# A three-layer fp32 network on one core: banks carried between phases, two split tiles on VectorE, an out projection cut four and four, and planned steps moved

## The chip, the cores and the metric

The kernel runs on one core of a Trainium2 chip. The metric is the device time of one launch in microseconds (us). Before the change three runs took 1080.02, 1081.88 and 1081.51 us, median 1081.51.

## What is computed

256 tokens of 1024 features, fp32, pass through three layers. Each has an RMS norm, an input projection, a mixer, an output projection added to x, a second norm, and a gated feed-forward network of width 2816 added to x.

```
layer 0: u = rms(x) @ w_in; o = silu(g) * rms(retention(q, k, v))        6 heads
layer 1: u = rms(x) @ w_in; o = rms(diff_attention(q, k, v, lam))        6 heads
both:    x += concat(o, memory_attention(rms(qc), mk, mv)) @ w_out       4 memory heads
layer 2: y_ssd = rms(ssd(conv4(xbc), dt) * silu(z)); y_fox = fox_attention(rms(q), rms(k), v)
         x += concat(y_ssd, y_fox) @ w_out                               16 + 16 heads
all:     x += (silu(gate) * value) @ w_down                              conv3 before it in layer 2
```

Layer 1's diff attention takes softmax p0 - lam * p1 of two score maps per head. All matrices are multiplied nearly exactly: weights and activations are each split into a rounded high part and a low part (the rest), and three of the four products are summed.

## The kernel before, in words

**Phases and tiles.** The program is a row of phases (PHASES): kv, and for each layer in, oa, ob, up, down. A phase walks weight tiles; an output of 128 features by 256 tokens needs one tile of 8 blocks (24 matmuls in `project`, L701 to L703, three per block) or, in oa and down, fewer or more blocks. Weights stream through a ring of four slots: SyncE loads a tile, ScalarE rounds it (`split_hi`, L1077), VectorE subtracts (`split_lo`, L1535), three tiles ahead of TensorE; SyncE reloads a slot when its low part is done.

**Banks.** Each output is summed in a PSUM bank. In in and oa phases outputs alternate between banks 0 and 1, in the other phases between 0 to 3, and each phase starts again at bank 0 (`phases`, `Phase.bank`). TensorE may start an output when VectorE has evacuated the last one in that bank. in0 and in1 have 17 outputs, in2 has 41, so these phases end in bank 0, and oa begins there.

**Out projection.** It runs in two phases: oa takes the inputs that are there early, ob the late ones. In layer 0 oa0 has six inputs (8 tiles of 6 blocks, 18 matmuls each) and ob0 two inputs, four outputs to a ring tile. In layer 1 it is four (8 tiles of 4 blocks) and four (two outputs to a ring tile). ob also computes the next norm's inputs: per output VectorE adds to x (L1633), ScalarE makes the high part and the square (L1082, L1088), GpSimd sums squares (L1460), VectorE makes the low part (L1541).

**The plan.** The mixer runs between tiles. `plans` gives for each layer and slot (one slot per ring tile of in, then of oa; slot 20 is the first of oa in layers 0 and 1, slot 45 in layer 2) a list of steps; every engine does its part of a step in list order. TensorE does its steps after the tile of the slot, or for the kinds in HALFWAY in the middle of the next tile. VectorE does the kinds in EARLY before it evacuates the slot's tile, MIDDLE after that and before the split, LATE after the split. ScalarE does its steps after its split of the slot. So one long wait on an engine holds all that is queued behind it, evacuations and splits too.

**Steps that matter here.** A `norm` is squares (ScalarE), sums (TensorE L809), roots by Ln and Exp (ScalarE L1211, L1213), five VectorE operations (L1724 to L1740), a `spread` (TensorE L818) and `norm_out` (VectorE L1752 or L1749). An attention unit is scores, maxima (VectorE L1788, L1799 or L1908), exponentials (ScalarE L1260, L1338), normalization (`softmax`, VectorE L1822 to L1835 and ScalarE L1280; `fox_probs`, L1915 and L1347), transposes of the weights (TensorE L944 or L917, copied by ScalarE L1270 or L1359), values (TensorE L843, L928, copied by VectorE L1848). `mix` splits one mixed tile into the inputs of the out projection: ScalarE rounds (L1294), GpSimd subtracts (L1488). `gated` is layer 0's product with silu(g) (L1779). In layer 2 `turn` transposes convolved tiles (TensorE L832), `small` prepares decays (its last step: TensorE L988), `z_silu` is one silu over eight tiles (L1372), and for head pair p come ssd_decay (L999, L1000, L1328), ssd_weights (VectorE L1887), ssd_out (TensorE L1011), ssd_skip (L1902), ssd_gate (L1926) and ssd_square. `fox_scores` is on TensorE L904 (fp32r), L908 (plain fp32), L911 (fp32r).

The pieces on which most hangs:

```
HALFWAY = ((), ("spread",), ("spread", "ssd_out"))
EARLY = {"norm_out", "softmax", "ssd_weights", "ssd_skip", "fox_probs"}
MIDDLE = {"group_out", "gated_soon"}
planned = sorted(planned, key=lambda step: step[0] in ("ssd_skip", "norm_out"))   # layers 1, 2, EARLY
```

Of the kernel before, what the change touches and what calls it, by code (L numbers as in the profile page):

```python
# [23 lines left out]
P = 128  # L24
T = 256
# [21 lines left out]
OUT_INPUTS = {"oa0": [6, 7, 0, 1, 2, 3], "ob0": [4, 5], "oa1": [6, 7, 0, 1], "ob1": [2, 3, 4, 5],  # L47
# [68 lines left out]
class Phase:  # L116
# [33 lines left out]
    def bank(self, i, c):  # L150

        return (self.out(i if type(i) is int else 0, c) - self.out0) % self.banks
# [11 lines left out]
def phases():  # L164

    at, out, all_, widths, bank_of = 0, 0, {}, [], []
    for name, n, blocks, body in PHASES:
        p = all_[name] = Phase(name, n, blocks, body, at, out)
        p.bank_of = bank_of
        bank_of += [j % p.banks for j in range(p.outs)]  # L170
# [5 lines left out]
def plans():  # L176
# [7 lines left out]
    def norm(layer, slot, tile, soon=False):  # L184
# [4 lines left out]
        plan[layer][slot + 2].insert(0, ("spread_soon" if soon or slot >= 20 and layer == 1 else "spread", tile))  # L189
# [14 lines left out]
    def mem_pairs(layer):  # L204

        for pair in range(2):
# [21 lines left out]
    norm(0, 15, 39)  # L228
    norm(0, 17, 41)
    for half_, slot, kind in ((0, 18, "gated"), (1, 19, "gated_soon"), (2, 20, "gated")):  # L230
        at(0, 20 if half_ == 2 else 18, "gate_silu", half_)
        at(0, slot, kind, half_)
    for half_, slot in ((0, 19), (1, 19), (2, 20)):
        at(0, slot, "mix", 2 * half_)
        at(0, slot, "mix", 2 * half_ + 1)


    for t, slot in ((18, 2), (0, 3), (6, 5), (2, 7), (8, 9), (4, 13), (10, 15), (8 + 64, 20)):
        norm(1, slot, t)
    norm(1, 16, 6 + 64, True)  # L240
    norm(1, 23, 10 + 64, True)
# [3 lines left out]
    for h, slots in enumerate(((9, 10, 11, 12), (11, 12, 13, 14), (13, 14, 15, 18), (15, 16, 17, 19),  # L245
                               (18, 19, 20, 21), (20, 21, 21, 22))):
# [4 lines left out]
        at(1, turned, "weights", "diff", h)  # L251
    for h, slot in enumerate((9, 11, 13, 15, 18, 20)):
        for m in range(2):
            at(1, slot, "scores", "diff", h, m)
    for k, slot in ((0, 19), (1, 19), (2, 23), (3, 23), (4, 26), (5, 26)):
        at(1, slot, "mix", k)


    for t in range(8):
        at(2, 3 + t, "turn", 8 + t)  # L260
    at(2, 13, "cb", 0)
    for s, slot in enumerate((13, 14, 14, 15, 15)):
        at(2, slot, "small", s)
    at(2, 21, "z_silu", 0)
# [10 lines left out]
    for j in range(4):  # L275
# [3 lines left out]
        for n in range(2):  # L279
# [3 lines left out]
            at(2, slot + 2, "fox_weights", p)  # L283
            at(2, slot + 3, "fox_values", p)
# [1831 lines left out]
```

## Time and profile before

| what | value |
|---|---|
| median of three runs | 1081.51 us |
| the profiled execution's own time | 1080.11 us |
| its span, first to last instruction | 1078.0 us |
| mean granted TensorE clock | 0.998 of full speed |
| TensorE busy (matmul) | 1046.7 us, 97% |
| VectorE busy | 746.3 us, 69% |
| ScalarE busy | 602.0 us, 56% |
| GpSimd busy | 165.7 us, 15% |
| read from HBM | 172.39 MB |

Busy time is the union of an engine's instructions. Matmuls are pipelined: one record is 0.28 us long, but in a full stream the next starts 0.12 us later. The distance of starts tells the pace. An idle time in square brackets stands before an instruction, with what ended it; "issue" means that nothing in the profile shows it. The profiled run is 1.4 us faster than the median.

### The profile page before, as it was taken

How to read it: one execution, taken by the hardware profiler on the slowest of the kernel's cores; microseconds unless marked ns; L12 is line 12 of the kernel's file. 1: busy time of each engine (PE TensorE's matmuls, PEld its weight loads, DVE VectorE, ACT ScalarE, POOL GpSimd, SP SyncE). 2: the span in 40 equal slices, each digit the busy share in tenths (PEclk: the TensorE clock that was granted, in tenths of full speed). 3: DMA queues.
4: the chain of work that ended last, by engine and by line, in shares of the span. 5: the costliest groups of instructions: out<-in, count | busy, mean ns of one | idle time of the engine just before them, and what ended most of it. 6: DMA issues, size and time to landing. Idle time of an engine off the chain costs nothing.

```text
span 1078.0 us, 23843 instructions
## 1 busy us (share of the span) xinstructions
PE 1046.7 (97%) x8638; PEld 1008.5 (94%) x8638; DVE 746.3 (69%) x1242; ACT 602.0 (56%) x1091; POOL 165.7 (15%) x172
## 2 busy tenths in 40 slices
PE   6999999999999998999999999999999999999998
PEld 6989999999999887899999998989888899999998
DVE  6875686666555887866665548867867479988743
ACT  7654564444544766654445446665766566666532
POOL 3200121111110000511111110000101033544300
PEclk9999999999999999999999999999999999999999
DMA  7533455555665332555555664534232355555563
GB/s 290 175 130 110 138 174 189 178 183 178 187 175 184 130 99 76 179 178 191 177 178 175 189 199 139 177 136 138 90 118 89 121 194 187 182 181 188 163 205 102
DMA packets 51479, 174.43 MB, mean 162 GB/s; under 512 B 5840, under 2 KB 7120, under 8 KB 51280
## 3 DMA queue, kind: packets, MB, share of 16 engines
q1 hardware_dynamic: 51408, 173.46, 49.9%
q8 instruction: 48, 0.79, 0.3%
q14 instruction: 23, 0.19, 0.1%
HBM read 172.39 MB, written 1.05 MB: 161 GB/s over the span
## 4 chain that ended last, share of the span: by engine, by line
PE 52%; DVE 5%; ACT 2%; issue 1%; POOL 0%; ACTq 0%; DVEq 0%
PE bank L701 10%; PE bank L702 9%; PE bank L703 9%; PE scores L703 6%; PE scores L702 6%; PE scores L701 6%; DVE ring_lo L1535 1%; ACT tmp L1338 1%; DVE xw_lo L1541 1%; PE scores L908 1%; PE bank L928 1%; PE scores L917 0%; DVE negmax L1908 0%; PE bank L1011 0%; PE bank L684 0%
## 5 line engine op out<-in xcount | busy, mean ns | idle before, releaser
L1535 DVE TENSOR_TENSOR ring_lo<-ring_raw,ring_hi 128x1024 fp32r<-128x1024 f32 (+2 forms) x338 | 402.0, 1192 | 59.1 <-ACT ring_hi L1077 53.2
L1077 ACT ACTIVATE ring_hi<-ring_raw 128x1024 fp32r<-128x1024 f32 (+2 forms) x338 | 341.3, 1012 | 87.2 <-PE bank L703 49.4
L701 PE MATMUL bank<-xw_hi,ring_hi 128*128 128x256 f32 x1048 | 303.2, 289 | 2.7 <-DVE ring_lo L1535 1.5
L702 PE MATMUL bank<-xw_lo,ring_hi 128*128 128x256 f32 x1048 | 296.3, 283 | 0.0
L703 PE MATMUL bank<-xw_hi,ring_lo 128*128 128x256 f32 x1048 | 296.2, 283 | 0.0
L701 PEld LDWEIGHTS bank<-xw_hi,ring_hi 128*128 128x128 f32 x1048 | 200.5, 191 | 9.7 <-issue 5.1
L702 PEld LDWEIGHTS bank<-xw_lo,ring_hi 128*128 128x128 f32 x1048 | 200.7, 191 | 0.2
L703 PEld LDWEIGHTS bank<-xw_hi,ring_lo 128*128 128x128 f32 x1048 | 200.6, 191 | 0.0
L701 PE MATMUL scores<-xw_hi,ring_hi 128*128 128x256 f32 x528 | 149.4, 283 | 0.0
L702 PE MATMUL scores<-xw_lo,ring_hi 128*128 128x256 f32 x528 | 149.4, 283 | 0.0
L703 PE MATMUL scores<-xw_hi,ring_lo 128*128 128x256 f32 x528 | 149.4, 283 | 0.0
L701 PE MATMUL bank<-act_hi,ring_hi 128*128 128x256 f32 x464 | 134.7, 290 | 11.3 <-DVE ring_lo L1958 7.4
L703 PE MATMUL bank<-act_hi,ring_lo 128*128 128x256 f32 x464 | 132.4, 285 | 0.0
L702 PE MATMUL bank<-act_lo,ring_hi 128*128 128x256 f32 x464 | 132.4, 285 | 0.0
L701 PEld LDWEIGHTS bank<-act_hi,ring_hi 128*128 128x128 f32 x464 | 90.1, 194 | 14.2 <-DVE ring_lo L1958 7.4
L701 PEld LDWEIGHTS scores<-xw_hi,ring_hi 128*128 128x128 f32 x528 | 101.4, 192 | 0.0
L702 PEld LDWEIGHTS scores<-xw_lo,ring_hi 128*128 128x128 f32 x528 | 101.4, 192 | 0.0
L703 PEld LDWEIGHTS scores<-xw_hi,ring_lo 128*128 128x128 f32 x528 | 101.4, 192 | 0.0
L1148 ACT ACTIVATE act_hi<-tmp 128x256 f32 (+1 forms) x66 | 27.2, 413 | 132.5 <-DVE tmp L1657 130.0
L1464 POOL TENSOR_TENSOR act_lo<-tmp,act_hi 128x256 f32 (+1 forms) x66 | 53.6, 812 | 264.1 <-ACT act_hi L1148 264.1
L702 PEld LDWEIGHTS bank<-act_lo,ring_hi 128*128 128x128 f32 x464 | 90.2, 194 | 0.0
L703 PEld LDWEIGHTS bank<-act_hi,ring_lo 128*128 128x128 f32 x464 | 90.1, 194 | 0.0
(236 smaller groups left out, 1773.8 us busy)
## 6 DMA issues: line engine op xcount, KB each, us to landing
ring_raw<-w_up SPq DMA_DIRECT2D x132, 512.0 KB, 3.2
ring_raw<-w_in SPq DMA_DIRECT2D x85, 512.0 KB, 3.2
ring_raw<-w_down SPq DMA_DIRECT2D x48, 512.0 KB, 3.6
ring_raw<-w_down SPq DMA_DIRECT2D x24, 384.0 KB, 3.8
ring_raw<-w_ob SPq DMA_DIRECT2D x10, 512.0 KB, 3.3
ring_raw<-w_oa SPq DMA_DIRECT2D x16, 256.0 KB, 2.7
ring_raw<-w_oa SPq DMA_DIRECT2D x8, 512.0 KB, 3.5
ring_raw<-w_kv SPq DMA_DIRECT2D x7, 512.0 KB, 6.6
```

What stands on the lines that cost most here:

```text
L701: mm(bank[b][:, 0:T], w_hi, tile(hi, t), start=kk == 0, stop=False)
L702: mm(bank[b][:, 0:T], w_hi, tile(lo, t), start=False, stop=False)
L703: last = mm(bank[b][:, 0:T], w_lo, tile(hi, t), start=False, stop=end)
L908: mm(bank[2 + n][:, a:a + width], u[r0:r0 + 64, q0 * T + it * P:q0 * T + (it + 1) * P], u[r0:r0 + 64, k0 * T:k0 * T + width], start=False, ...
L928: last = mm(bank[6][64 * n:64 * n + 64, q:T], tok(v_tok, (2 * p + n) * 64, 64, tt), fox_pt(n)[:, tt * T:tt * T + width], start=tt == 0, st ...
L1077: A(ring_hi[:, slot * DM:slot * DM + width], ring_raw[:, slot * DM:slot * DM + width], ACT.Copy).then_inc(hi_done, 1)
L1148: A(tile(act_hi, f), two(prod, h), ACT.Copy).then_inc(ffn_hi, 1)
L1338: last = A(fox_p(n)[:, a:a + width], bank[2 + n][:, a:a + width], ACT.Exp, bias=negmax[:, c:c + 1], accum_out=rowsum[:, c:c + 1])
L1464: G.tensor_tensor(tile(act_lo, f), two(prod, h), tile(act_hi, f).bitcast(f32), SUB).then_inc(ffn_lo, 1)
L1535: V.tensor_tensor(ring_lo[:, a:b], ring_raw[:, a:b], ring_hi[:, a:b].bitcast(f32), SUB).then_inc(lo_done, 1)
L1541: V.scalar_tensor_tensor(tile(lo, m), tile(src, m), pcol(name, m), tile(hi, m).bitcast(f32), MUL, SUB).then_inc(xl_done, 1)
```

## The change

Nothing is computed otherwise; steps are placed otherwise.

1. **Banks**: a phase begins with the bank after the last one of the phase before (`shift`).
2. **Out projection of layer 0**: four and four inputs, as in layer 1. oa0 has 12 matmuls to a tile, ob0 four ring tiles of two outputs.
3. **Low parts of mixed tiles in layers 0 and 1**: `mix` on single tiles becomes `mix_high` (ScalarE, two tiles at once) and `mix_low` (VectorE, two at once) in place of GpSimd. Layer 2 keeps `mix`.
4. **Layer 0**: spreads move to the middle of the next tile; the transposes of memory heads 0 and 2 too, their copy one slot later. The gate product of half 0 goes to slots 17 and 18 and its split to 18 and 19; halves 1 and 2 go to slots 20 to 23. `gate_silu` 0 brings the Ln and Exp table back, so there are two more table loads.
5. **Layer 1**: the first pair's split moves from slot 19 to 18. Head 5's scores on TensorE move from slot 20 to 19 and its maxima stay in 20; its transposes move from after tile 21 to the middle of tile 23, copy and values to slot 23. The norm of tiles 8 and 9 is spread and applied one slot later, that of tiles 10 and 11 in slot 26 instead of 25, before the split. Scores of head h wait for the maxima of the head before (VectorE) and not for its exponentials (ScalarE).
6. **Layer 2**: turns one slot later; the last small step in the middle of tile 16; ssd_gate not before slot 22, ssd_square not before 23. The EARLY order puts norm_out ahead of fox_probs where a slot has both. Transposes of fox pairs 6 and 7 move to the middle of the next tile, values of pair 7 one slot later. `fox_scores` does L908 before L904.

```diff
-          ("in0", 20, [8], 20), ("oa0", 8, [6], 8), ("ob0", 2, [8], 2), ...
+          ("in0", 20, [8], 20), ("oa0", 8, [4], 8), ("ob0", 4, [8], 4), ...
-OUT_INPUTS = {"oa0": [6, 7, 0, 1, 2, 3], "ob0": [4, 5], ...
+OUT_INPUTS = {"oa0": [6, 7, 0, 1], "ob0": [2, 3, 4, 5], ...
-        return (self.out(i if type(i) is int else 0, c) - self.out0) % self.banks
+        return (self.out(i if type(i) is int else 0, c) - self.out0 + self.shift) % self.banks
+        p.shift = (bank_of[-1] + 1) % p.banks if bank_of else 0
+        bank_of += [(j + p.shift) % p.banks for j in range(p.outs)]
...
-                at(layer, slot + 1 + n, "weights", "mem", 2 * pair + n)
+                if layer == 0 and n == 0:
+                    at(layer, slot + 1, "turned", "mem", 2 * pair)
+                    at(layer, slot + 2, "weights_copy", "mem", 2 * pair)
...
+    at(0, 18, "mix_high", 0)
     norm(0, 17, 41)
+    at(0, 17, "gate_silu", 0)
+    at(0, 18, "gated_early", 0)
+    at(0, 19, "mix_low_early", 0)
+    for half_ in (1, 2):
+        at(0, 20, "gate_silu", half_)
+        at(0, 20 + half_, "gated", half_)
+        at(0, 21 + half_, "mix_high", 2 * half_)
+        at(0, 21 + half_, "mix_low", 2 * half_)
...
-                               (18, 19, 20, 21), (20, 21, 21, 22))):
+                               (18, 19, 20, 21), (20, 21, 22, 23))):
+    for m in range(2):
+        at(1, 19, "scores_ahead", "diff", 5, m)
+        at(1, 20, "maxima", "diff", 5, m)
+    for k, slot in ((2, 24), (4, 26)):
+        at(1, slot, "mix_high", k)
+        at(1, slot, "mix_low", k)
...
-        at(2, 3 + t, "turn", 8 + t)
+        at(2, 4 + t, "turn", 8 + t)
-        at(2, a + 3, "ssd_gate", p)
-        at(2, max(a + 4, 22), "ssd_square", p)
+        at(2, max(a + 3, 22), "ssd_gate", p)
+        at(2, max(a + 4, 23), "ssd_square", p)
...
+            def mix_low(layer, k):
+                dve.wait_ge(pair_hi, number_low(layer, k) + 1)
+                t = mixed_tile(None, layer, k)
+                V.tensor_tensor(tile(act_lo, k, 2 * T), tile(u, t, 2 * T), tile(act_hi, k, 2 * T).bitcast(f32),
+                                SUB).then_inc(pair_lo, 1)
...
+            HALFWAY = (("spread", "turned"), ("spread", "turned"), ("spread", "ssd_out", "small_turn", "fox_turned"))
+                        probs_wait = any(step[0] == "fox_probs" for step in planned)
+                        last = ("ssd_skip", "fox_probs") if probs_wait else ("ssd_skip", "norm_out")
```

## Rows read from the trace of the kernel before

**Rows 1.** Page, parts 1 and 6: TensorE's busy time; loads of 256 KB, us to landing
```profile
PE 1046.7 (97%) x8638; PEld 1008.5 (94%) x8638; DVE 746.3 (69%) x1242; ACT 602.0 (56%) x1091; POOL 165.7 (15%) x172
...
ring_raw<-w_oa SPq DMA_DIRECT2D x16, 256.0 KB, 2.7
```

**Rows 2.** Waits of TensorE: waiting line <- releaser: us in total, times, longest
```profile
PE bank L809 <- DVE u L1752: 2.2, 3, 1.2
PE bank L944 <- ACT tmp L1280: 1.9, 1, 1.9
PE bank L1011 <- DVE con L1887: 1.8, 1, 1.8
PE bank L818 <- DVE root_parts L1740: 1.6, 3, 0.9
...
PE scores L917 <- ACT tmp L1347: 1.3, 2, 0.9
...
PE bank L944 <- DVE tmp L1828: 1.1, 1, 1.1
...
PE bank L988 <- DVE scratch L1872: 1.0, 1, 1.0
...
PE bank L832 <- issue: 0.8, 1, 0.8
```

**Rows 3.** Stretches, layer 0's tail, TensorE alone: length, busy (matmuls), clock, DMA, GB/s
```profile
117.50:120.00 2.50, 1.37 (x9) 0.99 0.14 22
120.00:122.50 2.50, 2.50 (x13) 0.50 0.34 135
122.50:125.00 2.50, 2.50 (x19) 0.83 0.20 54
```

**Rows 4.** Stretches: length, busy (count) of PE, PEld, DVE, ACT, POOL, clock, DMA, GB/s
```profile
126.00:140.00 14.00, 14.00 (x119) 14.00 (x118) 9.91 (x15) 6.41 (x8) 0.00 (x0) 1.00 0.72 225
144.00:149.00 5.00, 3.91 (x25) 3.15 (x25) 4.97 (x11) 4.12 (x9) 3.78 (x5) 1.00 0.33 105
454.00:458.00 4.00, 3.90 (x31) 3.56 (x30) 3.82 (x7) 3.19 (x6) 3.18 (x3) 1.00 0.49 165
419.00:444.00 25.00, 19.52 (x153) 16.68 (x152) 19.53 (x46) 15.53 (x35) 6.63 (x6) 1.00 0.43 139
```

**Rows 5.** Timeline of ScalarE, slot 20 of layer 0
```profile
118.92 0.62 ACT L1246 ACTIVATE u<-u 128x512 f32<-128x512 f32 x1
119.55 1.28 ACT L1061 ACT_TABLE_LOAD   x1
```

**Rows 6.** Timeline of VectorE, slots 21 and 22 of layer 1
```profile
429.22 0.36 DVE L1724 SCALAR_TENSOR_TENSOR bank<-bank,par,tmp 128x128 f32<-128x128 f32 x1 [0.53 <-ACT tmp L1213]
...
430.80 0.42 DVE L1848 COPY u<-bank 128x256 f32<-128x256 f32 x1
...
431.46 0.68 DVE L1535 TENSOR_TENSOR ring_lo<-ring_raw,ring_hi 128x512 fp32r<-128x512 f32 x1
```

**Rows 7.** Timeline of VectorE at the start of layer 2's turns
```profile
663.12 0.42 DVE L1663 TENSOR_TENSOR con<-bank,rstd 128x256 f32<-128x256 f32 x1 [0.27 <-PE bank L703]
```

**Rows 8.** Timeline of ScalarE, slot 21 of layer 2
```profile
720.18 1.91 ACT L1372 ACTIVATE u<-u 128x2048 f32<-128x2048 f32 x1
...
723.40 0.73 ACT L1328 ACTIVATE tmp<-bank,tmp 128x256 f32<-128x256 f32 x2
```

**Rows 9.** Timeline of VectorE, slot 20 of layer 2
```profile
722.19 0.42 DVE L1926 TENSOR_TENSOR u<-u 128x256 f32<-128x256 f32 x1 [3.74 <-ACT u L1372]
```

**Rows 10.** Timeline of ScalarE ahead of TensorE's longest wait at L809
```profile
770.74 0.64 ACT L1206 ACTIVATE tmp<-u 128x512 f32<-128x512 f32 x1
```

**Rows 11.** Timeline of TensorE, that wait
```profile
772.24 0.43 PE L809 MATMUL bank<-tmp,con 128*32 128x128 f32 x8 [1.20 <-DVE u L1752]
```

**Rows 12.** Timeline of TensorE, first two parts of one fox_scores
```profile
781.37 0.62 PE L904 MATMUL scores<-act_hi,pick_r 128*128 128x384 f32 x2
781.92 0.93 PE L908 MATMUL scores<-u 64*128 64x128 f32 x8
```

More of the change, by code:

```diff
@@ L188, in norm @@
         at(layer, slot + 1, "norm", tile)
-        plan[layer][slot + 2].insert(0, ("spread_soon" if soon or slot >= 20 and layer == 1 else "spread", tile))
+        plan[layer][slot + 2].insert(0, ("spread_soon" if soon else "spread", tile))
         if soon:
@@ L228, in plans @@
     norm(0, 15, 39)
+    at(0, 18, "mix_high", 0)
     norm(0, 17, 41)
[L230 to L238, printed above, removed]
+    at(0, 17, "gate_silu", 0)
[6 more added lines that the diff above has]
+        at(0, 21 + half_, "mix_low", 2 * half_)
+    for t, slot in ((18, 2), (0, 3), (6, 5), (2, 7), (8, 9), (4, 13), (10, 15)):
         norm(1, slot, t)
     norm(1, 16, 6 + 64, True)
-    norm(1, 23, 10 + 64, True)
+    for t, slot in ((8 + 64, 20), (10 + 64, 23)):
+        at(1, slot, "squares", t)
+        at(1, slot + 1, "norm", t)
+    plan[1][23].insert(0, ("spread", 8 + 64))
+    plan[1][24].insert(0, ("norm_out", 8 + 64))
+    at(1, 26, "spread_soon", 10 + 64)
+    at(1, 26, "norm_mid", 10 + 64)
     mem_pairs(1)
@@ L504, in program @@
                     k = (layer, *key)
-                    count("norm" if kind == "group_norm" else kind, (kind, *k) if kind in ("norm", "group_norm") else k)
+                    same = {"group_norm": "norm", "weights_copy": "weights", "maxima": "scores"}
+                    count(same.get(kind, kind), (kind, *k) if kind in ("norm", "group_norm") else k)
                     if kind == "norm":
@@ L901, in fox_scores @@
                 blocks_ = [(0, 0, P), (1, P, T)]
-                for n in range(2):
-                    pick = pick_r[:, 16 + 2 * p + n:17 + 2 * p + n].to_broadcast([P, P])
-                    mm(bank[2 + n][:, 0:T + P], pick, small_r[:, 0:T + P], start=True, stop=False)
                 for it, a, width in blocks_:
@@ L908, in fox_scores @@
                         mm(bank[2 + n][:, a:a + width], u[r0:r0 + 64, q0 * T + it * P:q0 * T + (it + 1) * P],
-                           u[r0:r0 + 64, k0 * T:k0 * T + width], start=False, stop=False)
+                           u[r0:r0 + 64, k0 * T:k0 * T + width], start=it == 0, stop=False)
+                for n in range(2):
+                    pick = pick_r[:, 16 + 2 * p + n:17 + 2 * p + n].to_broadcast([P, P])
+                    mm(bank[2 + n][:, 0:T + P], pick, small_r[:, 0:T + P], start=False, stop=False)
                 for n in range(2):
@@ L1294, in mix, with mix_high @@
                 A(tile(act_hi, k), tile(u, t), ACT.Copy).then_inc(mix_hi, 1)
+            def mix_high(layer, k):
+                t = mixed_tile(act, layer, k)
+                A(tile(act_hi, k, 2 * T), tile(u, t, 2 * T), ACT.Copy).then_inc(pair_hi, 1)
             def c_times_b(layer, _):
@@ L1941, in follow @@
                 return steps
-            EARLY = {"norm_out", "softmax", "ssd_weights", "ssd_skip", "fox_probs"}
-            MIDDLE = {"group_out", "gated_soon"}
+            EARLY = {"norm_out", "softmax", "ssd_weights", "ssd_skip", "fox_probs", "gated_early", "mix_low_early"}
+            MIDDLE = {"group_out", "norm_mid"}
             LATE = set(DO) - EARLY - MIDDLE
```

69 lines of the change are left out of this document (43 added, 26 removed), and 2 rows, old and new, of the table PHASES.

## Prediction

> **What bounds it now.** I read the page first. TensorE is busy for 1046.7 of 1078.0 us [rows 1], so the change can only win what lies in the other 31.3 us, plus what a matmul loses while it counts as busy. The number of matmuls stays the same: layer 0's out projection has 8 x 18 + 2 x 24 = 192 before and 8 x 12 + 4 x 24 = 192 after. VectorE (69%) and ScalarE (56%) are not the bound of the whole, but one of them ends most waits. So the second view is the list of TensorE's waits [rows 2]: eight entries that the change aims at, each some 1 to 2 us in total. The third is a table of stretches, since a wait can cost more than itself.
>
> That table has one surprise [rows 3]. In layer 0's tail the granted clock falls to 0.50, which is the lower of TensorE's two levels (1.2 instead of 2.4 GHz), after a stretch in which it worked for only 1.37 of 2.50 us. 9 + 13 + 19 = 41 matmuls take 7.5 us there. At full pace, 14.00 us for 119 matmuls or 0.118 us each [rows 4], they take 4.8. So 2.7 us are lost, 1.1 as idle time (2.50 - 1.37) and 1.6 by the clock. By the Trainium skill ("TensorE: Matmul & The Clock Gate", Part 1) the clock follows how busy the engine has been, which agrees with these rows.
>
> **Layer 0.** (a) oa0's first tile needs four inputs instead of six, the split of the pair it lacks is moved ahead into slots 18 and 19, and oa0 begins in the bank that in0 left free. The 2.7 us go, and I add 0.4 for the bank, between nothing and the 0.8 that a wait on nothing visible takes elsewhere [rows 2]. What comes back: ScalarE's slot 20 now holds two silus and two table loads. A load takes 1.28 and a silu 0.62 us [rows 5], with its split 4.4 us in all, while a tile of 12 matmuls takes 12 x 0.118 = 1.4. The split for tile 24 is queued behind that, VectorE's low part behind the split, and behind this the evacuation of tile 22, the gate products and both low parts. TensorE reaches tile 24 some 6.1 us after oa0's start, VectorE frees its bank some 0.5 later, and the two products and two low parts of 0.6 us each hold tile 25 for some 0.7 more. I take 1.2 back; the ends are 0 and 2.7. Net 1.9. By the Trainium skill ("ScalarE: Activation LUTs", What ACT_TABLE_LOAD costs) each switch takes about 2.66 us with its drain. The row has 1.28 with the next instruction 1.3 after; by the page slot 20 would be 2.8 us longer, and the total some 2.8 us higher.
> (b) up0's start is VectorE-bound: 144 to 149 us holds 25 matmuls in 5.0 us (2.1 lost), while up1 after four-input groups holds 31 in 4.0 (0.3 lost) [rows 4]. ob0 gets layer 1's shape, so 1.7 us is won. SyncE issues two loads more; loads of 256 KB land in 2.7 us [rows 1], and each has four tiles, 5.7 us, from its slot's release to its use. I cost them at nothing, with that distance as their cover; without it each would show its 2.7.
> (c) The transposes of memory head 0 wait 1.1 us for VectorE [rows 2]. Half a tile later they don't, but their copy now stands behind a split on ScalarE and the next transposes want that bank: 0.3 back, net 0.8 (ends 0 and 1.1). Spreads in the middle of a tile win some 0.3 of the 1.6 at L818 [rows 2]; the rest is layer 1's.
> Layer 0: 1.9 + 1.7 + 0.8 + 0.3 = 4.7.
>
> **Layer 1.** From 419 to 444 us TensorE is busy 19.52 of 25 us: 5.5 us of waits [rows 4]. All seem to be removed, but VectorE is busy 19.53 of the same 25 and gets two low parts more in it, some 0.6 each by the 0.68 of a low part of the same width [rows 6]. I walked its queue. Head 5's scores move ahead, so its maxima, exponentials and softmax end some 1.5 us sooner. Then the norm of tiles 8 and 9 (waits 0.53 for ScalarE's roots, 429.22), head 4's values (430.80) and only then the evacuation and split (431.46) follow in the old order [rows 6]. TensorE, with its transposes moved away, now arrives early and waits there: about 0.5 for the bank of tile 21, 1.3 for head 4's values to leave bank 6, and, since the last norm is applied in slot 26 behind an evacuation and its low part behind a 1024-wide split, 1.6 in ob1's first output. That makes some 3.4 of which pipelining hides part of what it hid before; the difference I take is 3.0 (ends: 0.5, if VectorE's added 1.2 and a later last norm eat the rest, and 5.5). Head 5's wait on maxima instead of exponentials adds no wait: maxima come first.
>
> **Layer 2.** (d) Turns. The first waits 0.8 us [rows 2], for the copy of the norm's roots that VectorE makes in slot 3. A slot later that is done. But from there VectorE idles only 0.27 us per slot or less [rows 7]: TensorE's lead runs into convolutions that aren't ready, and each turn waits for ScalarE's copy of the one before. I take 0.5 (ends 0 and 0.8).
> (e) The last small step waits 1.0 us at L988 [rows 2] and moves 12 matmuls, 1.4 us, back: 1.0 (ends 0.5 and 1.0). Its copies on ScalarE are wanted only in slot 17.
> (f) ssd_out waits 1.8 us at L1011 [rows 2]. ScalarE's silu over eight tiles ends at 722.09 [rows 8], and VectorE stands 3.74 us before ssd_gate, with ssd_weights queued behind it [rows 9]. With the gate in slot 22 VectorE goes on. Late next is ssd_decay 5 on TensorE, which wants the exponential of decay 4, queued on ScalarE behind silu and load and done at 724.13 [rows 8], when TensorE arrives at about 723.8: 0.4 back, net 1.4 (ends 0.5 and 1.8).
> (g) norm_out ahead of fox_probs: 2.2 us at L809 in three waits [rows 2]. The longest ends at 772.24 and began 1.20 sooner, at 771.04 [rows 11]. But L809 also wants the squares, which end at 771.38 [rows 10], so only 0.8 of 1.2 goes; the others, 0.5 each, go: 1.8. Late fox_probs cost nothing, since ScalarE's next work is a split.
> (h) Fox transposes 6 and 7: 1.3 us [rows 2] in two waits, of which 0.1 stays behind the same ScalarE work: 1.1 with some for the values (ends 0.6 and 1.3).
> (i) Order in fox_scores. L904's two matmuls of 384 columns should take 2 x 1.5 x 0.118 = 0.35 us and take 0.55 before L908 starts [rows 12]: a change between fp32r and plain fp32 costs some 0.1 to 0.2. Seven of eight fox_scores follow plain fp32 values, and with L908 first they change once instead of three times: 7 x 0.17 = 1.2 (ends 0 and 2.4).
> Layer 2: 0.5 + 1.0 + 1.4 + 1.8 + 1.1 + 1.2 = 7.0.
>
> **Sum.** 4.7 + 3.0 + 7.0 = 14.7 us. The profiled execution took 1080.11, so it would take 1065.4; it is 1.4 faster than the median 1081.51, which gives 1066.8. I put the forecast between the two: 1066.
>
> **Rivals.** 1. VectorE is the bound of both tails. For: 19.53 of 25 us busy, and added work. Against: GpSimd's 6.63 us in that stretch [rows 4] go in part, and VectorE idles where it waits for ScalarE. Price: layer 1 keeps 0.5, (a) 0.5, (c) 0, (d) 0, (g) to (i) half: 1.7 + 0.5 + 0.5 + 0.3 + 1.0 + 1.4 + 2.0 = 7.4, time 1074.
> 2. No new waits: layer 0 gives 2.7 + 0.4 + 1.7 + 1.1 + 0.3 = 6.2, layer 1 5.5, layer 2 0.8 + 1.0 + 1.8 + 2.2 + 1.3 + 2.4 = 9.5: 21.2 us, time 1060. Against it is the queue on VectorE.
> 3. Slower: the clock stays at its lower level through both out projections. The waits that I leave in slots 24 and 25 of layer 0 and in slots 22 to 28 of layer 1 come again with nearly every tile. 13 matmuls in 2.50 us are 0.192 each against 0.118 [rows 3, 4], near the lower level's double; 192 matmuls in each tail cost 14 us, both 28, and 28 - 14.7 is 13 slower, 1094. [...] Against: my waits are 1.6 of several us at most, and layer 1's 5.5 of 25 us did not lower it [rows 4]. [...]
> 4. The longer table load of the page: 1069, inside the forecast's range.
> 5. The change doesn't do what it says: the low part isn't earlier because ScalarE's mix_high waits for a late norm_out. Then only layer 2 and (b) hold: 8.7, time 1073, near rival 1.
>
> **Chances.** Forecast 0.60, rival 1 (with 5) 0.20, rival 2 0.11, rival 3 0.03, rival 4 0.06. The range, 1060 to 1075, holds all but rival 3 and the edges. A measurement of this kernel tells about 0.2%, 2.2 us, from no change. Faster by over that: 0.95; within 0.02, slower 0.03.
>
> **What would show it.** In the changed profile: clock 1.00 all through layer 0's tail; the wait for GpSimd's act_lo in oa0 gone; up0's start at layer 1's pace; waits at L1011, L988 and L809 gone or under 0.6; a wait of some 1.5 us in ob1's first output, now on VectorE's low part; L908 straight after L928. I am wrong if a stretch of out projection shows a clock under 0.9, if VectorE's splits (ring_lo) come to lead TensorE's waits, or if TensorE's busy time plus idle time falls by less than 7.

## The result, and the profile after

The changed kernel takes **1065.94 us** (median of four runs, 1065.02 to 1066.21), the kernel before 1081.70 (four runs beside it, 1080.02 to 1082.60). The ratio is 0.9855, interval 0.9838 to 0.9872: 15.8 us less, where the forecast was 1066. The profiled execution took 1066.21 us with a span of 1064.4, 13.9 us less than the profiled execution before. The other 1.9 us have a likely source in the clock. Of 35 executions of the kernel before that were timed beside the experiments, 18 have a mean granted clock of 0.997 and take 1082.1 us on average, 14 have 0.998 (the profiled one too) and take 1080.6, and two have 1.000 and take 1079.3. The changed kernel has 1.000 in all four.

The page of the changed kernel, parts 1 and 2 (the clock in 40 slices) and part 6 (loads of up and ob; the last number is us to landing):

```profile
PE 1042.4 (98%) x8638; PEld 1007.9 (95%) x8638; DVE 749.8 (70%) x1250; ACT 604.4 (57%) x1089; POOL 155.9 (15%) x160
...
PEclk9999999999999999999999999999999999999999
...
ring_raw<-w_up SPq DMA_DIRECT2D x132, 512.0 KB, 3.2
...
ring_raw<-w_ob SPq DMA_DIRECT2D x12, 512.0 KB, 4.1
```

The span is 1078.0 - 1064.4 = 13.6 us shorter. TensorE is busy 4.3 us less with the same 8638 matmuls [rows 1], so 9.3 are idle time. Where it went is best read from stretches cut at the same instructions in both kernels. The cuts are the starts of the mean squares (L743 before, L780 after), of oa and ob (the first matmul that reads act_hi, and L724 or L761), of the product of C and B (L839, L876), and of decays 0 and 7 (L999, L1036). In this order the stretches are: in0; oa0 with ob0; in1; oa1; ob1; layer 2's turns; its small steps; decays 0 to 7; and the rest up to the next mean square.

Three of these stretches in the kernel before (oa0 with ob0, oa1, the turns): length, busy TensorE (matmuls), clock, share of the DMA engines' time, GB/s.

```profile
116.96:148.94 31.98, 29.35 (x216) 0.95 0.49 157
...
420.07:441.49 21.42, 17.82 (x142) 1.00 0.42 133
...
648.91:691.83 42.92, 41.45 (x334) 1.00 0.46 156
```

The same three in the changed kernel, and the last one.

```profile
114.77:144.51 29.74, 27.83 (x223) 1.00 0.63 196
...
415.55:433.94 18.39, 16.20 (x137) 1.00 0.45 143
...
641.35:684.46 43.11, 40.89 (x335) 1.00 0.46 158
...
723.23:873.47 150.24, 148.73 (x1257) 1.00 0.40 129
```

| stretch | before, us | after, us | won | forecast |
|---|---|---|---|---|
| in0: memory transposes, spreads, and the 0.4 for the bank | 77.17 | 74.85 | 2.3 | 1.5 |
| oa0 and ob0: the rest of (a), and (b) | 31.98 | 29.74 | 2.2 | 3.2 |
| layer 1: in1 | 80.25 | 80.16 | 0.1 | |
| oa1 | 21.42 | 18.39 | 3.0 | 3.0, all of layer 1 |
| ob1 | 16.54 | 16.53 | 0.0 | |
| turns (d) | 42.92 | 43.11 | -0.2 | 0.5 |
| small steps (e) | 14.41 | 13.35 | 1.1 | 1.0 |
| decays 0 to 7, the gate (f) | 26.93 | 25.42 | 1.5 | 1.4 |
| the rest: norm's output, fox transposes, fox order (g, h, i) | 153.84 | 150.24 | 3.6 | 4.1 |
| sum | | | 13.7 | 14.7 |

One line has the wrong sign, and equal sums can hide opposite errors (layer 1 does). in1 and oa1 have to be read together: the change moves head 5's scores, about 1.0 us of TensorE's work, from oa1 into in1 (80.16 us with them there, 79.11 in the experiment below that puts head 5 back), and the 0.87 us that TensorE waited for a bank at the end of in1 are gone. TensorE's waits of the changed kernel (waiting line, releaser: us in total, times, longest), as far as the steps speak of them:

```profile
PE bank L738 <- DVE x L1658: 2.1, 3, 0.9
PE bank L869 <- ACT x_tok L1265: 2.0, 4, 1.2
PE scores L761 <- DVE act_lo L1831: 1.4, 1, 1.4
PE bank L880 <- ACT tmp L1308: 1.1, 1, 1.1
...
PE bank L846 <- ACT tmp L1244: 0.6, 1, 0.6
PE bank L983 <- ACT tmp L1308: 0.3, 1, 0.3
...
PE bank L1048 <- DVE con L1939: 0.2, 1, 0.2
PE bank L855 <- DVE root_parts L1785: 0.2, 1, 0.2
PE scores L956 <- ACT tmp L1391: 0.2, 1, 0.2
```

Against [rows 2], with the line in the changed kernel first: L846 (L809 before) from 2.2 to 0.6, L983 (L944) from 3.0 in two to 0.3, L1048 (L1011) from 1.8 to 0.2, L855 (L818) from 1.6 to 0.2, L956 (L917) from 1.3 to 0.2; the 1.0 at L988 is gone, and so are the waits for GpSimd (1.4 in two at L701 and 1.0 at L724). New are the first four rows. L869 is the turn: from one wait of 0.8 to four, of 2.0 together.

### The profile page after: what moved, and what is told of

The parts are those of the page before. It is cut to its first block, busy times and chain, and to the rows that moved or that the text cites. A ratio compares the mean times of both kernels' runs of the same rounds, so it can differ in the third digit from the quotient of the medians.

```text
span 1064.4 us, 23813 instructions
## 1 busy us (share of the span) xinstructions
PE 1042.4 (98%) x8638; PEld 1007.9 (95%) x8638; DVE 749.8 (70%) x1250; ACT 604.4 (57%) x1089; POOL 155.9 (15%) x160
## 4 chain that ended last, share of the span: by engine, by line
PE 51%; DVE 6%; ACT 3%; issue 1%; ACTq 0%; DVEq 0%
PE bank L738 10%; PE bank L739 9%; PE bank L740 9%; PE scores L738 6%; PE scores L740 6%; PE scores L739 6%; DVE ring_lo L1580 1%; ACT tmp L1382 1%; DVE xw_lo L1586 1%; PE scores L944 0%; PE bank L1048 0%; PE bank L967 0%; DVE negmax L1960 0%; DVE tmp L1717 0%; DVE x L1678 0%
## 5 line engine op out<-in xcount | busy, mean ns | idle before, releaser
L738 PE MATMUL bank<-xw_hi,ring_hi 128*128 128x256 f32 x1048 | 302.6, 289 | 1.9 <-DVE ring_lo L1580 0.6
L738 PEld LDWEIGHTS bank<-xw_hi,ring_hi 128*128 128x128 f32 x1048 | 200.5, 191 | 8.4 <-issue 5.1
L738 PE MATMUL scores<-xw_hi,ring_hi 128*128 128x256 f32 x528 | 150.1, 284 | 0.1
L738 PE MATMUL bank<-act_hi,ring_hi 128*128 128x256 f32 x448 | 129.6, 289 | 9.9 <-DVE ring_lo L2013 7.4
L739 PE MATMUL bank<-act_lo,ring_hi 128*128 128x256 f32 x448 | 127.8, 285 | 0.0
L740 PE MATMUL bank<-act_hi,ring_lo 128*128 128x256 f32 x448 | 127.6, 285 | 0.0
L738 PEld LDWEIGHTS scores<-xw_hi,ring_hi 128*128 128x128 f32 x528 | 101.4, 192 | 0.4 <-DVE xw_lo L1586 0.3
L738 PEld LDWEIGHTS bank<-act_hi,ring_hi 128*128 128x128 f32 x448 | 86.8, 194 | 11.8 <-DVE ring_lo L2013 7.4
L739 PEld LDWEIGHTS bank<-act_lo,ring_hi 128*128 128x128 f32 x448 | 87.0, 194 | 0.0
L740 PEld LDWEIGHTS bank<-act_hi,ring_lo 128*128 128x128 f32 x448 | 86.9, 194 | 0.0
```

Of the source, the lines that this page charges most:

```text
L738: mm(bank[b][:, 0:T], w_hi, tile(hi, t), start=kk == 0, stop=False)
L739: mm(bank[b][:, 0:T], w_hi, tile(lo, t), start=False, stop=False)
L740: last = mm(bank[b][:, 0:T], w_lo, tile(hi, t), start=False, stop=end)
```

## The experiments

### The turns: one slot back, and in the middle of a tile

```diff
-        at(2, 4 + t, "turn", 8 + t)
+        at(2, 3 + t, "turn", 8 + t)        # both kernels
-            ... ("spread", "ssd_out", "small_turn", "fox_turned"))
+            ... ("spread", "ssd_out", "small_turn", "fox_turned", "turn"))    # the second only
```

> The changed kernel with layer 2's turns back in slots 3 to 10. My theory of step (d): after the first turn the stretch is paced by VectorE's convolutions and by ScalarE's copy of the turn before, so the place of the turns hardly matters. From up to the first product of C and B (layer 2's mean square to L1054's kind) the kernel before took 42.9 us and the changed one 43.1; I expect 42.9 here, all later stages as in the changed kernel, total 0.2 us less. Rival (the forecast's step): moving them had won 0.5 to 0.8, then this run is slower by that.

> The changed kernel with each turn in the middle of the next tile (8 to 15 after slots 3 to 10). Theory: a turn waits for ScalarE's copy of the turn before, which comes half a tile too late; with 1.4 us more distance the four waits (2.0 us as idle time, 2.6 in starts) go, and the stretch is limited by TensorE: about 41.0 instead of 43.1 us, total 1.5 to 2.5 us less. Rival: VectorE's convolutions (3.1 us of work per slot against 3.3) are the limit and hold it at 42.5 or more.

**Measured.** One slot back: 1065.51 us (1065.16 to 1065.92), ratio 0.9863 (0.9847 to 0.9880). From the mean square to the product of C and B it takes 42.92 us (640.49 to 683.41), 0.2 less than the changed kernel and the same as before. In the middle: 1062.62 us (1062.38 to 1063.35), ratio 0.9836 (0.9820 to 0.9853), and that stretch is 40.38 us (640.65 to 681.03), 2.7 less. Timeline of TensorE in the changed kernel, the first of the four turns that wait (start, length, and in brackets the idle time before it); the other three wait 0.28 us each:

```profile
658.53 0.41 PE L869 MATMUL bank<-con,u 128*128 128x128 f32 x2 [1.15 <-ACT x_tok L1265]
```

**What follows.** The move took away the first turn's wait of 0.8 us and gave the second turn one of 1.15, for another engine. The transposes of one turn want the bank that ScalarE's copy of the one before leaves, and that copy is queued behind the convolution's silu. Every second turn waits in this way (the second, fourth, sixth and eighth). Half a tile (1.4 us of matmuls) is enough cover: with the turns in the middle no wait at L869 is left at all.

### Layer 1: who does the low parts, and head 5

```diff
-                  "maxima": scores, "norm_mid": norm_out, "mix_low": mix_low, "mix_low_early": mix_low,
+                  "maxima": scores, "norm_mid": norm_out,      # VectorE; mix_low runs on GpSimd, one tile at a time
```

> The changed kernel with the low parts of mixed tiles in layers 0 and 1 on GpSimd again (two of 256 columns each), at the same places of the plan. Theory: a pair takes GpSimd 1.5 to 1.7 us against VectorE's 0.7, but VectorE is freed of it. In layer 0's oa the two waits for banks (0.75 and 0.47) shrink to at most 0.4 in all: oa0 13.7 us goes to 12.9. In layer 1 the last pair is wanted at once: ob1's wait of 1.4 us becomes some 2.0, and the first pair's place makes no wait. Total within 0.5 us of the changed kernel. Rival (VectorE is the bound of both tails): 2 us or more faster. Second rival (the low parts on VectorE are the gain of the change): 2 us or more slower.

```diff
+    norm(1, 20, 8 + 64)
+    norm(1, 23, 10 + 64, True)
...
-                               (18, 19, 20, 21), (20, 21, 22, 23))):
+                               (18, 19, 20, 21), (20, 21, 21, 22))):
...
-    for m in range(2):
-        at(1, 19, "scores_ahead", "diff", 5, m)
-        at(1, 20, "maxima", "diff", 5, m)
...
-    for k, slot in ((2, 24), (4, 26)):
+    for k, slot in ((2, 23), (4, 26)):
```

> The changed kernel with layer 1's head 5 and its two last normalisations put back to their old tiles; the low parts stay pairs on VectorE, and the banks and everything in layers 0 and 2 stay changed. The changed kernel won 3.1 us in layer 1, all of it in the first part of the out projection. If the earlier scores and turned weights of head 5 and the later normalisation are what won it (my theory): layer 1 goes from 115.1 back to 117.6 to 118.2, with waits of 1 to 2 us again at head 5's scores and weights and ahead of the ring's high part, and the time is 1068.5 to 1069. If the pairs on VectorE won it (rival): layer 1 stays below 116 and the time is 1066 to 1067.

**Measured.** Low parts on GpSimd: 1069.54 us (1067.75 to 1069.68), ratio 0.9899 (0.9883 to 0.9916), 3.6 slower in the median. Head 5, both norms and the middle pair's slot back, the pairs still on VectorE: 1065.72 us (1065.18 to 1066.36), ratio 0.9854 (0.9839 to 0.9869): no slower than the changed kernel. TensorE's timeline in layer 1's out projection, first the kernel before:

```profile
420.07 0.35 PE L701 MATMUL bank<-act_hi,ring_hi 128*128 128x256 f32 x1 [0.87 <-issue]
421.38 0.39 PE L701 MATMUL bank<-act_hi,ring_hi 128*128 128x256 f32 x1 [0.35 <-POOL act_lo L1488]
428.65 0.55 PE L944 MATMUL bank<-con,tmp 128*128 128x128 f32 x3 [1.94 <-ACT tmp L1280]
430.94 0.66 PE L818 MATMUL bank<-root_parts,spread_r 128*128 128x128 f32 x4 [0.32 <-DVE root_parts L1740]
438.07 0.66 PE L818 MATMUL bank<-root_parts,spread_r 128*128 128x128 f32 x4 [0.91 <-DVE root_parts L1740]
444.13 0.39 PE L724 MATMUL bank<-act_hi,ring_hi 128*128 128x256 f32 x1 [1.04 <-POOL act_lo L1488]
```

The same waits with head 5 and the norms back:

```profile
422.05 0.55 PE L971 MATMUL bank<-con,tmp 128*128 128x128 f32 x3 [1.94 <-ACT tmp L1306]
424.34 0.66 PE L843 MATMUL bank<-root_parts,spread_r 128*128 128x128 f32 x4 [0.32 <-DVE root_parts L1773]
431.46 0.66 PE L843 MATMUL bank<-root_parts,spread_r 128*128 128x128 f32 x4 [0.91 <-DVE root_parts L1773]
```

The changed kernel has three others in their place, all in the list of its waits above: 0.92 at L738 (the longest of its three), 1.11 at L880 and 1.39 at L761.

**What follows.** My theory fell. Head 5's old waits are there again (1.94 + 0.32 + 0.91 = 3.17 us) and layer 1 still takes no longer: 114.80 us between its mean squares (335.31 to 450.12) against 115.08 (335.39 to 450.47) and 118.21 before (339.82 to 458.03). So moving head 5 and the norms exchanged 3.17 us of waits for 0.92 + 1.11 + 1.39 = 3.42 and won nothing. The 3.4 us between this kernel and the one before are what it keeps of the change: the banks, the first pair's split one slot earlier, the pairs on VectorE, and scores that wait for maxima. No run takes these apart in full. The banks alone win nothing here (the experiment below). With the pairs on GpSimd TensorE doesn't wait for a low part at oa1's start either, so what took away the first two waits is the banks with the earlier slot; VectorE's part shows at ob1. The waits at the bank and for GpSimd account for 0.87 + 0.35 + 1.04 = 2.26 of them; the other 1.1 are matmuls that stood closer together (busy 112.2 before, 111.2 here). In the GpSimd kernel the last pair's low part is late for ob1's first output,

```profile
437.47 0.38 PE L761 MATMUL scores<-act_hi,ring_hi 128*128 128x256 f32 x1 [3.05 <-POOL act_lo L1540]
```

3.05 instead of 1.39 us, and layer 1 is 1.6 longer (116.67 us). That is VectorE's part in the changed kernel. The other 2 us of the median are not in the profiled execution, the fastest of the four at 1067.75 us with a mean granted clock of 1.000. The other three took 1069.44 to 1069.68 with 0.998, so a fall of the clock accounts for them; where it fell isn't known. It also settled a side question. Layer 0's waits at L738 stayed (0.75 and 0.41 us, against 0.75 and 0.47), so VectorE's added work is not their cause.

### The order in fox_scores

```diff
-                for it, a, width in blocks_:        # plain fp32 scores first
...
+                for n in range(2):                  # the picks in fp32r first, as before the change
+                    pick = pick_r[:, 16 + 2 * p + n:17 + 2 * p + n].to_broadcast([P, P])
+                    mm(bank[2 + n][:, 0:T + P], pick, small_r[:, 0:T + P], start=True, stop=False)
```

> The changed kernel with fox_scores in the old order (fp32r, plain fp32, fp32r). Theory: two changes between fp32r and plain fp32 more for seven of eight, 0.17 us for each fox_scores, so the time from the first fox_scores to the last norm is longer by 1.2 us. Rival: the order costs nothing (0.0 to 0.3), and what layer 2 gained there came from norm_out and the transposes.

**Measured.** 1066.46 us (1066.30 to 1067.32), ratio 0.9872 (0.9856 to 0.9889). The picks first (this experiment), from the picks to the next tile (L738):

```profile
770.53 0.62 PE L943 MATMUL scores<-act_hi,pick_r 128*128 128x384 f32 x2
771.08 0.93 PE L947 MATMUL scores<-u 64*128 64x128 f32 x8
...
772.28 0.28 PE L738 MATMUL bank<-xw_hi,ring_hi 128*128 128x256 f32 x1
```

The scores first (the changed kernel):

```profile
771.35 0.93 PE L944 MATMUL scores<-u 64*128 64x128 f32 x8
772.21 0.62 PE L948 MATMUL scores<-act_hi,pick_r 128*128 128x384 f32 x2
...
772.90 0.28 PE L738 MATMUL bank<-xw_hi,ring_hi 128*128 128x256 f32 x1
```

**What follows.** 772.28 - 770.53 = 1.75 us against 772.90 - 771.35 = 1.55: 0.2 for one fox_scores. From the end of the first fox_scores (L950) to the next mean square the sum is 1.3 us (133.32 against 132.04), for 1.2 forecast. Step (i) holds in size. Its mechanism is likely: the matmuls are the same ones in another order, with two changes between fp32r and plain fp32 more or less, but no run has another order with the same number of changes.

### Parts of the change by themselves, in the kernel before

Only the banks and the later gate:

```diff
-        return (self.out(i if type(i) is int else 0, c) - self.out0) % self.banks
+        return (self.out(i if type(i) is int else 0, c) - self.out0 + self.shift) % self.banks
-        at(2, a + 3, "ssd_gate", p)
+        at(2, max(a + 3, 22), "ssd_gate", p)
```

> The kernel before with two parts alone, in stages that don't touch: banks carried on (ends of in), and ssd_gate and ssd_square moved (layer 2, slots 20 to 23). Gate: from the first ssd_decay to the eighth the kernel before takes 26.9 us; my step (f) says 1.4 less, 25.5; the rival, that ssd_decay 5 then waits as long, 26.9. Banks: in layer 1 the 0.9 us ahead of oa goes, if the first pair's low parts, split by GpSimd in slot 19, don't take its place: I expect 0.3 of it to be left to win, since they are ready only 0.6 us later. In layer 0 the low parts are late anyway: no gain, and the clock falls to its lower level in oa0 again, since the wait is only moved. Total: 1.5 to 2 us less than before.

Only the four-and-four cut of layer 0 and VectorE's EARLY order:

```diff
-("oa0", 8, [6], 8), ("ob0", 2, [8], 2)
+("oa0", 8, [4], 8), ("ob0", 4, [8], 4)
-                        planned = sorted(planned, key=lambda step: step[0] in ("ssd_skip", "norm_out"))
+                        last = ("ssd_skip", "fox_probs") if probs_wait else ("ssd_skip", "norm_out")
```

> The kernel before with two other parts alone: the out projection of layer 0 in four and four inputs (mixed tiles where they were), and the EARLY order with norm_out ahead of fox_probs. Four and four: up0's start gets 1.7 to 2 us shorter by my step (b); in oa0 the waits for bank and GpSimd stay, so if it is they that lower the clock, it falls again, and of the 2.7 us of step (a) nothing is won; total for layer 0 about 1.7. Rival: six inputs made the waits, with four the clock stays at 1.00 and layer 0 wins over 3 us. Order: by step (g) 1.8 us between the eighth ssd_decay and the last norm. Total 3.5 us less; by the rival 5 or more.

**Measured.** 1078.72 us (eight runs, 1077.74 to 1079.14), ratio 0.9976 (0.9966 to 0.9987), and 1078.30 us (ten runs, 1077.78 to 1080.59), ratio 0.9973 (0.9964 to 0.9983). The gate alone wins its 1.5 us (decays 0 to 7 in 25.4 us). The banks alone win nothing in a tail, not even the 0.3 us that I expected in layer 1 (118.19 us against 118.21); in0 is 0.56 us shorter, and oa0 with ob0 0.9 longer. Layer 0's first wait is now one, and longer than the 0.42 and 1.06 us of before,

```profile
119.11 0.38 PE L702 MATMUL bank<-act_hi,ring_hi 128*128 128x256 f32 x1 [1.67 <-POOL act_lo L1489]
```

and the clock falls as in [rows 3]:

```profile
120.00:122.50 2.50, 2.41 (x12) 0.68 0.40 139
122.50:125.00 2.50, 2.50 (x16) 0.63 0.16 24
```

With four and four the same low parts are late, in smaller pieces (0.20 and 0.52 us, beside 0.42 and 0.55 for banks). The clock stays at 1.00 there, against my expectation, and layer 0 takes 106.49 us between its mean squares instead of 109.15. So the cut alone is worth 2.7 us in this execution, 1.6 of them the clock's by the prediction's sum. oa0 takes 13.58 us with it, against 13.73 in the changed kernel: there the pair's earlier split and the banks win nothing on top of the cut. They exchange these waits for the 0.75 and 0.47 us at L738. And in this kernel the clock fell somewhere new. Stretches of TensorE with the cut and the order:

```profile
722.50:725.00 2.50, 2.50 (x14) 0.50 0.54 159
725.00:727.50 2.50, 2.50 (x19) 0.81 0.31 77
```

The kernel before, with the same wait of 1.80 us at L1011:

```profile
722.50:725.00 2.50, 1.46 (x13) 1.00 0.00 0
```

Decays 0 to 7 took 28.47 us there, 1.5 more than the 26.93 of before. The order of the norm's output is read behind this, from decay 7 to the mean square: 153.15 against 153.84 us, only 0.7. Of 1.8 us of waits at L809 that go (2.2 to 0.4), 0.7 come back as three short waits elsewhere.

### The norm's order and the memory transposes, taken out of the changed kernel

```diff
-                        last = ("ssd_skip", "fox_probs") if probs_wait else ("ssd_skip", "norm_out")
+                        planned = sorted(planned, key=lambda step: step[0] in ("ssd_skip", "norm_out"))
-                    at(layer, slot + 1, "turned", "mem", 2 * pair)
-                    at(layer, slot + 2, "weights_copy", "mem", 2 * pair)
+                at(layer, slot + 1 + n, "weights", "mem", 2 * pair + n)
```

> The changed kernel with two parts undone in places far apart. VectorE's order with the norm's output and the probabilities in layer 2 as before: the prediction's 1.8 us if its step is right also in this kernel, 0.7 us as the same order showed in the kernel before alone (rival); read from the eighth decay of layer 2 to the next mean square, now 150.2 us. The memory heads' transposes back from the middle of a tile to its end in layers 0: the prediction's 0.8 us, read from layer 0's first mean square to the start of its out projection, now 74.9 us (77.2 before). The time: 1068.5 with the prediction's numbers, 1067.4 with the rival's.

**Measured.** 1067.89 us (1067.73 to 1068.50), ratio 0.9874 (0.9859 to 0.9889), 1.95 slower than the changed kernel. Its waits that are new against the changed kernel:

```profile
PE bank L842 <- DVE u L1793: 2.4, 3, 1.4
...
PE bank L979 <- DVE tmp L1876: 1.5, 1, 1.5
```

Its stretch in0 takes 76.06 us (40.27 to 116.33), and the one from decay 7 to the mean square:

```profile
724.65:875.76 151.11, 148.35 (x1257) 1.00 0.40 128
```

**What follows.** The memory transposes are worth 76.06 - 74.85 = 1.2 us (forecast 0.8), the order 151.11 - 150.24 = 0.9 (forecast 1.8). In the second stretch the waits grew by 1.4 us net (2.4 against the 0.6, 0.2 and 0.2 of L846, L855 and L1048), but the matmuls were busy 148.35 instead of 148.73: part of a wait comes back as closer matmuls behind it.

### Queues of ScalarE and VectorE

The changed kernel with the turns in the middle; the second reload of the Ln and Exp table moved from slot 20 to just before ob0; in layer 1 head 5's softmax behind the split, and values ahead of a norm:

```diff
-                if n != 1:
+                if n == 0:
                     ln_and_exp()
...
                 run(f"oa{layer}", follow(layer, PH[f"in{layer}"].n))
+                if layer == 0:
+                    ln_and_exp()
...
-            plan[1][soft].insert(0, ("softmax", "diff", h, 1 - m))
+            plan[1][soft].insert(0, ("softmax_late" if h == 5 else "softmax", "diff", h, 1 - m))
```

> The changed kernel with turns in the middle of the next tile and two moves that change no amount of work. Layer 0: the table load that brings Ln and Exp back goes from slot 20 to just ahead of ob0. Layer 1: head 5's softmax after the evacuation and split of slot 21 in place of ahead of them, and head 4's values copied by VectorE before the norm of tiles 8 and 9. Theory: the waits left in both tails come from the order in the queues, not from VectorE's load. Layer 0's waits for banks (0.75 and 0.47) go to 0.3 or less; layer 1's 0.9 (bank) goes and its 1.1 (values) becomes 0.5: total 2 to 3 us below the run with turns moved alone (1062.6). Rival, VectorE is the bound of these tails: the waits come back at other places and the total stays within 0.7.

The same, and the last pair's low part and norm ahead of the split:

```diff
-    at(1, 26, "norm_mid", 10 + 64)
+    at(1, 25, "norm_mid", 10 + 64)
-        at(1, slot, "mix_low", k)
+        at(1, slot, "mix_low" if k == 2 else "mix_low_mid", k)
```

> As e7, and layer 1's last norm is applied in slot 25, before the split, and the last pair's low parts in slot 26 before the split. Theory: the wait in ob1's first output (1.4 us) shrinks by 0.8, total 3 to 4 us below 1062.6. Rival: the split that is pushed back makes ob1's first tile late by as much, total as e7.

> The same kernel as the one with the order of the queues changed, a second look: there TensorE's clock fell to 0.50 behind a wait of 1.7 us in layer 1 and layer 1 took 116.9 us. If the fall belongs to that wait, it is there again, in the same stretch and with the same 116.9 us; if it is chance from run to run, the clock stays at 1.00 and layer 1 takes 115.5 us, as in the kernel with the last pair moved, with the same wait or not.

**Measured.** 1063.10 us (1062.53 to 1063.57), ratio 0.9830 (0.9815 to 0.9845); with the last pair 1063.41 (1062.66 to 1064.84), ratio 0.9839 (0.9825 to 0.9852); the first once more, one run, 1062.61. The turns alone had brought 1062.62, so both kernels missed the 2 to 4 us less that I had expected, and the totals are the rivals'. In layer 0 both waits at L738 are gone, and oa0 takes 12.3 instead of 13.7 us. ScalarE's timeline there in the changed kernel:

```profile
115.68 1.28 ACT L1284 ACT_TABLE_LOAD   x1
116.98 1.16 ACT L1284 ACTIVATE u<-u 128x512 f32<-128x512 f32 x2
118.15 1.28 ACT L1099 ACT_TABLE_LOAD   x1
119.44 1.15 ACT L1115 ACTIVATE ring_hi<-ring_raw 128x512 fp32r<-128x512 f32 x2
```

Without the second load the splits start at 117.81 us instead of 119.44. In layer 1 new waits stand in for the old ones: 1.67 us at head 5's transposes and 0.75 at the values behind them. In the first profiled execution the clock fell behind these two,

```profile
422.50:425.00 2.50, 1.75 (x12) 0.91 0.13 52
425.00:427.50 2.50, 2.50 (x14) 0.50 0.34 115
```

and in that of the repeated run, with waits of 1.67 and 0.76 us, it didn't:

```profile
422.50:425.00 2.50, 1.74 (x12) 1.00 0.27 108
425.00:427.50 2.50, 2.22 (x19) 1.00 0.34 106
```

Layer 1 took 116.94 us the first time and 115.78 the second.

**What follows.** The table load explains layer 0's remaining waits: 1.4 us. In layer 1 a better order of VectorE's queue for head 5 doesn't help; its softmax is a chain across three engines, and what is put ahead of it comes out as a wait behind it. The fall of the clock is chance from execution to execution: the same waits brought it once and not the other time. The four executions of the first kernel have a mean granted clock of 0.998, 1.000, 0.998 and 1.000.

### What beats both kernels

The turns, the table load and the last pair, with head 5's softmax where the change puts it:

> The changed kernel with the turns in the middle of tiles (as in the kernel that took 1062.6 us), the second reload of the table moved to just before layer 0's second part of the out projection, and in layer 1 the last two low parts and norm moved ahead of the phase's last output, with head 5's softmax left where the change puts it and only value head 4 put before a norm on VectorE. If the causes add: layer 0 gains 0.9 against the kernel with the turns alone (its first part 12.3 instead of 13.7 us), layer 1 up to 0.8 (the wait of 1.4 us for the low part gone), no new wait of over 1 us at head 5's transposes: 1061 us, and no fall of the clock. If head 5's chain is the limit in layer 1 and a wait only moves: layer 1 stays at 115 and the time is 1062.

**Measured.** **1061.69 us** (five runs, 1061.11 to 1062.37), ratio 0.9819 (0.9805 to 0.9832), 4.3 us under the changed kernel. Its out projections, oa0 with ob0, and ob1:

```profile
114.08:142.71 28.63, 27.58 (x222) 1.00 0.64 204
...
432.16:448.09 15.93, 15.57 (x120) 1.00 0.58 199
```

Between the two profiled spans (1064.4 and 1059.3) lie 5.1 us: 2.7 from the turns, 1.1 from layer 0's 28.63 against 29.74 us, 0.6 from ob1's 15.93 against 16.53, and 0.7 ahead of the first mean square, where nothing was changed. It missed the 0.9 that I had expected of layer 0 against the kernel with the turns alone (103.48 against 103.89 us): oa0 won its 1.4, but ob0 up to the mean square took 16.3 instead of 15.3. That stretch is 15.2 to 16.0 us, 15.6 on average, in the changed kernel and the five experiments that leave layer 0's out projection as it is, and 15.9 to 16.3, 16.0 on average, in the four with the table load moved to its start. There VectorE stands behind the load, waiting for ScalarE's high part:

```profile
131.19 0.48 DVE L1588 SCALAR_TENSOR_TENSOR xw_lo<-x,par,xw_hi 128x256 fp32r<-128x256 f32 x1 [0.89 <-ACT xw_hi L1120]
```

That wait is 0.81 to 0.89 us in the four and 0.16 to 0.54 in the six. So of the 1.4 us that the moved load wins in oa0 some 0.4 come back in ob0; the rest of the spread are loads from HBM that land early or late (step (b) below). Head 5's old places together with these three moves weren't tried.

## Why the prediction was right, point by point

**The total** was off by less than 0.1 us, the sum against the profiled executions by 0.8 (1065.4 forecast, 1066.21 measured). That the first is so small is in part luck. The steps are off by +0.8 (in0), -1.0 (oa0 and ob0), -0.7 (turns) and -0.5 (the last stretch), which cancel in part, and the forecast lay midway between two values, 1065.4 and 1066.8, with no reason given for the middle. No rival came about; the second, no new waits at all, is what the three moves of the last experiment approach. Of the signs named in advance one did not come: up0's start at layer 1's pace (see (b)).

**(a) holds in size.** The wait for GpSimd's act_lo is gone, the clock is 1.00, and 0.75 + 0.47 = 1.22 us came back for the 1.2 that I took, for the reason given: ScalarE's slot with two silus and two table loads. By the Trainium skill ("ScalarE: Activation LUTs", What ACT_TABLE_LOAD costs) the table load with its drain would have been twice as long; here the silu starts 1.30 us after the load does, so the row was right to take. What the prediction didn't separate is the cut from the rest. With the cut of four and four alone the clock stayed at 1.00 too and oa0 took 13.58 us, so in oa0 the cut is the whole gain, and the earlier split with the banks only changed whom TensorE waits for. Since the fall of the clock is chance, one execution of that kernel doesn't show that the cut prevents it.

**(b) is too large.** Of 1.7 us some 0.7 came in this execution and 1.2 on average. oa0 and ob0 won 2.2 us here (16.0 us from ob0 to the mean square) and 2.7 with the average of 15.6; (a) is 1.5 of it once its bank is counted in in0. The term that failed is "I cost them at nothing" for the loads. The loads of w_ob in layer 0 landed 5.0 us after issue (median of four), not in the 2.7 of a smaller load. My cover was 5.7 us, and in it a tile must also be rounded (1.06 us) and get its low part (1.23 us). ScalarE's rounding of the third of ob0's four tiles, first in the changed kernel, then with the turns one slot back, where layer 0 is the same and the median landing was 4.4 us:

```profile
129.75 1.06 ACT L1115 ACTIVATE ring_hi<-ring_raw 128x1024 fp32r<-128x1024 f32 x1 [1.47 <-DMA ring_raw<-w_ob]
```

```profile
128.92 1.06 ACT L1115 ACTIVATE ring_hi<-ring_raw 128x1024 fp32r<-128x1024 f32 x1 [0.49 <-DMA ring_raw<-w_ob]
```

Both kernels begin ob0 within 0.01 us of each other. From this tile on VectorE is 0.8 us later in the first, evacuations included, and the stretch takes 16.0 us instead of 15.2. The five us ahead of the next mean square hold 30 matmuls in the first [rows 4: 25 before] and 38 in the second.

**(c) is too small by 0.4:** the memory transposes are worth 1.2, above my upper end of 1.1, which was the wait itself. Without the move the wait in the changed kernel is 1.5. The rest of in0's 2.3, 1.1, are the bank and the spreads, 0.7 forecast; the bank is 0.56 of it where the banks were changed alone.

**Layer 1: the size is right (3.0, measured 3.1), the account of it is half wrong.** The three new waits were forecast at 0.5, 1.3 and 1.6 us and came at 0.92, 1.11 and 1.39, at the named places. But I had set the 5.5 us of waits against them as one block. Head 5's and the norms' part of that, 3.2, paid for the new waits and no more; what was won are the 2.3 us at the bank and for GpSimd's low parts, and closer matmuls. The step that failed is "Head 5's scores move ahead, so its maxima, exponentials and softmax end some 1.5 us sooner" as a reason for a gain.

**(d) failed in sign:** +0.5 forecast, -0.2 measured. "A slot later that is done" is true of the norm's roots, and the first turn no longer waits. But "each turn waits for ScalarE's copy of the one before" was in my text but not priced: 1.15 + 3 x 0.28 = 2.0 us of waits.

**(e), (f), (h), (i)** hold: 1.1 for 1.0, 1.5 for 1.4, 0.2 of 1.3 left at L956, 1.3 for 1.2. No run undoes (h) alone; of the last stretch's 3.6 us the order (0.9) and fox_scores (1.2 in that stretch) leave 1.5 for it, where 1.1 was forecast.

**(g) is half:** 0.7 in the kernel before, 0.9 in the changed one, for 1.8. I took the waits that go at L809 for time won. With the cut and the order alone 0.4 of them stayed, for the squares as predicted, and 0.7 of small new waits came beside them.

## What to carry to other kernels

When a block of waits is to be removed by several edits at once, price each edit by the waits that only it removes; a sum can be right while one of the edits does nothing. A short step of TensorE that needs another engine's copy is best put in the middle of the next tile, since moving it a whole slot only changes whom it waits for. Count a table load in the queue in which it stands: 1.3 us ahead of a split reached TensorE whole, and moved to another full place some 0.4 us of it came back there. And count with a load not only its landing but the rounding and the low part that must follow before TensorE can use the tile.

## What the runs showed of the hardware that I had not expected

- The clock's fall is not a function of the wait. A wait of 1.80 us at L1011 left it at 1.00 in the kernel before and sent it to 0.50 in one with the same instructions around; 1.67 with 0.75 us lowered it in one execution and not in the next of the same kernel. Each fall cost 1.2 to 1.6 us. By the Trainium skill ("TensorE: Matmul & The Clock Gate", Part 1) the point at which the clock rises at the start varies from run to run of one kernel. These runs show such variation in the middle of a kernel too, where it decides whether the clock falls at all.
- TensorE loses about 0.1 us at each change between fp32r and plain fp32 matmuls, an estimate from the 0.2 us that one fox_scores gains by two changes less (1.75 against 1.55 us).
- Four loads of 512 KB issued within 5.2 us land in 3.3 to 5.3 us each, where the median over the launch for w_up is 3.2, and with that the same ob0 takes 15.2 to 16.0 us from execution to execution.
